# A long convolution's skip connection: on GpSimd in two passes ahead of its product with the gate, or on VectorE

## The reference, cut to what matters

```
def bidir_long_conv(z, h_freq, skip):
    n = z.shape[1]
    zf = z.astype(jnp.float32)
    y = jnp.fft.irfft(jnp.fft.rfft(zf, n=2 * n, axis=1) * h_freq, n=2 * n, axis=1)[:, :n]
    return (y + zf * skip.astype(jnp.float32)).astype(z.dtype)
...
    vb, x1, x2 = jnp.split(hb, 3, axis=-1)
    z = x1 * bidir_long_conv(vb, h_freq[:, 0], skip[0])
    z = x2 * bidir_long_conv(z, h_freq[:, 1], skip[1])
```

## Time and profile before

| | |
|---|---|
| median of 3 runs | 3538.1 us (3537.11 to 3541.84) |
| the profiled execution, its own time | 3541.32 us |
| its span in the profile | 3539.5 us |
| mean granted TensorE clock | 0.961 |
| busy in the span: PE, DVE, ACT, POOL | 3195.3, 1913.3, 1130.4, 112.9 us |
| the edited stage (first fold to last gate product) | 1990.69 to 2166.49 us |

### The profile page before, as it was taken

One profiled execution on the slowest core, in us unless ns is written; L12 is line 12 of the kernel. 1 busy time (PEld: TensorE's weight loads), 2 busy tenths in 40 slices (PEclk: granted clock), 3 DMA queues, 4 the chain that ended last, 5 costly groups with the idle time before them and its releaser, 6 DMA issues. The chain is left out here.

```text
span 3539.5 us, 39517 instructions
## 1 busy us (share of the span) xinstructions
PE 3195.3 (90%) x15464; PEld 2498.6 (71%) x15464; DVE 1913.3 (54%) x2964; ACT 1130.4 (32%) x2065; POOL 112.9 (3%) x114
## 2 busy tenths in 40 slices
PE   6998898798889888989899897799999989989997
PEld 4876665565668663469788566688888867767875
DVE  4648698844765686642434598624234255543333
ACT  3346323254332542332122122321111134532221
POOL 0000000100100000000000021000000000000000
PEclk9999899899999998989999999899999999999998
DMA  4223311321322232221111225322222111122221
GB/s 145 85 59 126 119 48 60 131 71 36 133 100 90 66 113 111 92 86 48 48 72 48 82 72 189 144 72 91 76 72 92 51 56 25 65 76 95 95 91 52
DMA packets 57153, 299.20 MB, mean 85 GB/s; under 512 B 8375, under 2 KB 8631, under 8 KB 31080
## 3 DMA queue, kind: packets, MB, share of 16 engines
q1 hardware_dynamic: 52504, 280.87, 22.4%
q0 software_dynamic: 4496, 16.26, 1.5%
HBM read 269.05 MB, written 15.73 MB: 80 GB/s over the span
## 5 line engine op out<-in xcount | busy, mean ns | idle before, releaser
L410 PE MATMUL bank<-high,slot_high 128*128 128x512 f32 (+1 forms) x3344 | 1236.4, 370 | 122.1 <-DVE low L334 78.2
L411 PE MATMUL bank<-low,slot_high 128*128 128x512 f32 (+1 forms) x3344 | 1225.1, 366 | 0.0
L412 PE MATMUL bank<-high,slot_low 128*128 128x512 f32 (+1 forms) x3344 | 1221.4, 365 | 0.0
L390 DVE TENSOR_TENSOR slot_low<-slot,slot_high 128x2048 fp32r<-128x2048 f32 (+1 forms) x172 | 390.4, 2270 | 1050.7 <-ACT slot_high L384 1050.6
L410 PEld LDWEIGHTS bank<-high,slot_high 128*128 128x128 f32 x3344 | 633.5, 189 | 259.9 <-issue 118.4
L384 ACT ACTIVATE slot_high<-slot 128x2048 fp32r<-128x2048 f32 (+1 forms) x172 | 325.7, 1895 | 1352.0 <-PE bank L412 1159.3
L411 PEld LDWEIGHTS bank<-low,slot_high 128*128 128x128 f32 x3344 | 635.5, 190 | 109.1 <-issue 4.5
L412 PEld LDWEIGHTS bank<-high,slot_low 128*128 128x128 f32 x3344 | 633.4, 189 | 108.0
L1066 DVE TENSOR_REDUCE peak<-bank 128x1 f32<-128x128 f32 (+2 forms) x224 | 109.1, 507 | 135.9 <-PE bank L1195 48.4
L1118 ACT ACTIVATE prob<-bank,peak_bias 128x128 f32<-128x128 f32 (+2 forms) x224 | 119.8, 542 | 71.0 <-DVE peak_bias L1074 70.9
L449 PE MATMUL bank<-slot_high,low 128*128 128x256 f32 x448 | 125.7, 280 | 0.0
(11 more groups left out here) (381 smaller groups left out, 3837.2 us busy)
## 6 DMA issues: line engine op xcount, KB each, us to landing
slot<-in_gu SPq DMA_DIRECT2D x44, 1024.0 KB, 4.7
slot<-in_a_in SPq DMA_DIRECT2D x32, 1024.0 KB, 4.8
mod_raw<-in_mod SPq DMA_DIRECT2D x44, 512.0 KB, 5.0
slot<-in_e_rest SPq DMA_DIRECT2D x16, 1024.0 KB, 4.8
slot<-in_down SPq DMA_DIRECT2D x16, 1024.0 KB, 4.7
a_value<-in_mod SPq DMA_DIRECT2D x24, 512.0 KB, 3.4
spectra<-f_spectrum SPq DMA_DIRECT2D x12, 1024.0 KB, 3.8
h_spectrum<-spectra SPq DMA_DIRECT2D x12, 1024.0 KB, 4.9
```

What stands on the lines that cost most here:

```text
L390: dve.tensor_tensor(k.slot_low[s][:, 0:n], k.slot[s][:, 0:n], k.slot_high[s][:, 0:n].bitcast(F32), ALU.subtract).then_inc(k.low[s], 1)
L410: pe.matmul(out, wh, xh, start=kt == 0, stop=False)
L411: pe.matmul(out, wh, xl, start=False, stop=False)
L412: mm = pe.matmul(out, wl, xh, start=False, stop=kt == self.kt - 1)
```

## The change

The skip connection leaves VectorE. GpSimd makes it in two passes: it scales the tile's input into a new buffer `h_passed` (a `tensor_scalar`), which it may do before the tile is evicted, but not before the previous tile's addition is done; when the tile has been evicted it adds `h_passed` to it (a `tensor_tensor`); then it makes the product with the gate as before. VectorE's list has only the multiplies left, in the same order. TensorE, ScalarE and SP keep their lists.

```diff
+        passed, passed_on = k.sb("h_passed", BANK, ctx), k.named("skip_scaled")
...
-            def skip(e, j):
-                n, c, o, half = items[e]
-                r, tile = 4 * e + j, half * 4 + j
-                dve.wait_ge(scaled.sem, scaled.at(r + 1))
-                dve.scalar_tensor_tensor(result[r % 4][:, 0:n], place(tile, c, n), k.v("h_skip", o * KT + tile),
-                                         result[r % 4][:, 0:n], ALU.mult, ALU.add).then_inc(skipped.sem, 1)
-
-            for f in range(H[0]):
-                multiply(0, f)
             for e in range(count):
-                left = list(range(4))
-                for f in range(H[e + 1] if e + 1 < count else 0):
-                    multiply(e + 1, f)
-                    for _ in range(2):
-                        skip(e, left.pop(0))
-                for j in left:
-                    skip(e, j)
+                for f in range(H[e]):
+                    multiply(e, f)
 
         @block.gpsimd
         def _(pool):
             for e, (n, c, o, half) in enumerate(items):
                 for j in range(4):
                     r, tile = 4 * e + j, half * 4 + j
+                    if r:
+                        pool.wait_ge(skipped.sem, skipped.at(r))
+                    pool.tensor_scalar(passed[:, 0:n], place(tile, c, n), k.v("h_skip", o * KT + tile), None, ALU.mult)\
+                        .then_inc(passed_on.sem, 1)
+                    pool.wait_ge(passed_on.sem, passed_on.at(r + 1))
+                    pool.wait_ge(scaled.sem, scaled.at(r + 1))
+                    pool.tensor_tensor(result[r % 4][:, 0:n], result[r % 4][:, 0:n], passed[:, 0:n], ALU.add)\
+                        .then_inc(skipped.sem, 1)
                     pool.wait_ge(skipped.sem, skipped.at(r + 1))
                     pool.tensor_tensor(place(tile, c, n), result[r % 4][:, 0:n], place(8 * (o + 1) + tile, c, n),
                                        ALU.mult).then_inc(out_ready.sem, 1)
```

More of the change, by code:

```diff
@@ L3282, in long_conv @@
     k.end(u, loaded=32, pair_full=2 * g, pair_free=2 * g, odd_copied=2 * g, spectrum_step=6 * g, frequencies_ready=g,
-          output_scaled=4 * count, skip_added=4 * count, sequence_ready=4 * count,
+          output_scaled=4 * count, skip_scaled=4 * count, skip_added=4 * count, sequence_ready=4 * count,
           spectrum_loaded0=16 * ((g + 1) // 2), spectrum_loaded1=16 * (g // 2))
```

## The result

The changed kernel takes 3567.9 us (median of 4 runs, 3566.97 to 3568.3); beside it on the same chip the kernel before takes 3540.0 (3537.11 to 3544.64, 4 runs). The ratio is 1.0077, with a 95% interval of 1.006 to 1.0095: 0.77% slower. The profiled execution took 3568.3 us itself, its span is 3566.3.

The account below looks back on a forecast made before the run. In the edited stage VectorE bounds stretches 1, 3, 5 and TensorE 2, 4. Terms 4.6 + 10.7 + 5.7 + 2.4 (tail) + 3.4 (clock) = +26.8 us on 3538.1: 3565 us, 0.76% slower, range 3550 to 3580.

Parts of the forecast that it names:

- What bounds each stretch: Edited stage, cut into six spans at engine handovers: VectorE bounds spans 1, 3, 5; TensorE 2, 4; the sixth is the tail.
- stretches 1, 3 and 5: VectorE's spans: first fold to item 1's last pack, item 3's fold to item 5's pack, item 7's fold to last pack.
- What the skips cost on the path: 32 skips leaving VectorE save 3.7 us in stretch 1 and 6.9 in stretch 3, together 10.6, nothing elsewhere.
- stretches 2 and 4: TensorE's spans, 19.17 and 19.15 us: inverse transform, then next item's forward transform; 7.5 us of room each for VectorE.
- The hold of a two-input GpSimd operation: Each one meeting a VectorE operation with two SBUF inputs delays VectorE 1.0 us at 512, 0.45 at 256.
- "not slower" case: Rival: the multiply's long tensor_tensor isn't held by GpSimd, so only the skips' removal counts; 3538 us, chance 0.09.
- The scaling: GpSimd's tensor_scalar pass, taken as 0.90 us at 512 and 0.51 at 256, holding VectorE 0.62 and 0.25.
- How often: Share of GpSimd operations falling on VectorE instructions that read twice from SBUF: 0.79, giving 8.3 or 3.6 us per item.
- The tail: Stretch 6, last pack to last gate product on GpSimd, 7.57 us before; forecast 10.0, so +2.4.
- GpSimd becomes the bound: Rival: GpSimd's work plus waits outlasts the stage, ScalarE and TensorE then wait; priced +40, 3578 us, chance 0.16.
- the prediction's own signs: L3232 to L3253 mean up about 0.4 us; scaling 0.5 to 1.3; evictions waiting for GpSimd would show GpSimd as bound.
- The clock: TensorE restarts at a lower clock after waiting: 1.7 us each in stretches 2 and 4, +3.4, lower end 0.

## Why the forecast came out

**What bounds each stretch: right.** VectorE is busy 51.80 of 53.94, 73.26 of 73.92 and 15.86 of 16.29 us in stretches 1, 3 and 5; with TensorE's clock kept up, stretch 2 takes its old 19.17 us, though VectorE's work in it grew: the room was there.

**What the skips cost on the path: right as a length, but not as a gain.** 3.7 us forecast in stretch 1, 3.5 gained without any skip; 6.9 in stretch 3, where 2.0 are gained beside 4.2 us of holds. But of such a gain TensorE takes back 4.2 us in stretches 2 and 4, because its own list isn't done sooner, and the gate products, no longer released by a skip between two multiplies, take back the rest. The prediction names TensorE's cap for the case that nothing is held; in its sum the 10.6 us are taken off whole. Since the holds were larger than that gain, VectorE stayed behind TensorE and the sum isn't hurt by it.

**The hold of a two-input GpSimd operation: right,** 1.10 and 0.53 us at 512 and 256 for 1.0 and 0.45. The multiply is held as the prediction said from L837 and the skips, and the "not slower" case falls with L3233's 1434 ns.

**The scaling: mis-sized in both of its sides.** I took 0.90 and 0.51 us, with 1.28 and 0.72 as the upper bound ("With one input it lies between"). It takes 1.56 and 0.92, outside the bounds: fewer inputs did not make it shorter than the two-input operation. Its hold is 0.41 and 0.20, not 0.62 and 0.25, so "its own length less 0.27" doesn't hold for it. Beside VectorE it waits for two turns. The lower estimate beside that sum, 0.6 and 0.4 us, falls further short.

**How often: too high.** 84 operations by the last pack and a share of 0.79 make 44.0 us of holds (4 x 8.3 + 3 x 3.6); measured, 34.3. By the last pack GpSimd had made about 75 of its 96 operations (21 stand in the tail's row). At the measured holds these would make, for 16 tiles of 512, 8 of 256 and one more of 256, 41.8 + 10.1 + 1.3 = 53 us if each fell on VectorE; 34.3 is 0.65 of that. The share forgot that GpSimd also runs while VectorE is idle, as at 2066.55 in stretch 2, and that it can be kept out until the folds come, as at 2027.63. How much of the difference each makes isn't shown.

**The tail: the term that failed.** +2.4 us forecast, +9.9 measured. I let GpSimd be idle when the last item's first tile was evicted. It was an item behind: 7.4 us of item 6 were left at the last pack, then four tiles of 2.5. That is the mechanism of the rival "GpSimd becomes the bound", which was priced for the whole stage (+40) and given 0.16; it held, but for the last item only. ScalarE did wait for GpSimd's products (10.6 us in four), and by the kernel with more buffers little or nothing of that reached the path. By the prediction's own signs two of its cases held at once: L3233 grew, and evictions waited for GpSimd. Two of its signs came out otherwise: the mean of the ten long ones and packs grew by 0.29 us, not 0.4 or so, and the scaling lies outside 0.5 to 1.3.

**The clock: right in one place of two.** 2.6 us in stretch 2 for 1.7, behind a wait of 3.68; nothing in stretch 4, where TensorE waited 1.53 us and not the 10.7 that I had put. The price came from one wait of 3.56 us, and a wait of 3.55 in the changed kernel cost nothing, so part of this term is luck.

**The total is luck.** The 26.8 is a sum in which +7.5 for the tail stands against -7.5 for all else. The direction and the two mechanisms, holds and queue, were forecast; that the number hit is cancellation.

## What to carry to other kernels

Moving VectorE work to an idle GpSimd is not free when that work reads SBUF and VectorE runs instructions with two SBUF inputs: here each such meeting cost VectorE 1.1 us at 128x512, more than the 0.74 us skip that was moved. Cost the receiving queue as if it were a bound: add up its operations with their waits, see where it stands when the stage ends, and put what it is behind into the tail. And ask what the next engine lets you gain: leaving the skips out altogether gained nothing, since TensorE was 0.3 us from being the bound at item 1 and the gate products met the multiplies instead.

## What the runs showed of the hardware beyond what I expected

- A GpSimd read can be kept out for ten VectorE instructions in a row: 9.94 us for work of 1.27, with each VectorE instruction at its full speed. In the changed kernel itself no operation took over 3.6; its first addition was kept out through four packs (3.42 for 1.27). SBUF — State Buffer in the Trainium skill, "Who interferes with whom", says of VectorE's two-port modes that whoever issues first gets the shared ports for the whole instruction, and the other blocks. Taken over to two SBUF inputs, GpSimd would wait for one instruction; here ten finished before it got in. The measurement decides.
- A scaling of one input by a factor per partition on GpSimd takes 1.56 us at 128x512, longer than a product of two tensors (1.27); with a constant it took 1.48. The GPSIMD Engine Reference of the Trainium skill, "4.1 Engine selection", calls one-input work roughly line-rate; these rows don't show it.
- The factor per partition costs GpSimd one more wait beside VectorE (3.58 for 2.46 us), and holds VectorE no longer.
- GpSimd memsets of 440 to 755 columns beside the multiplies left their 1.22 us untouched.
